# Two unused 64-byte buffers, one ahead of and one behind the halves of the down and mixer weights

## The reference

```
def swiglu(h, w_gate, w_up, w_down):
    return (jax.nn.silu(h @ w_gate) * (h @ w_up)) @ w_down
```

## Time and profile before

| what | before |
|---|---|
| median of three runs | 1358.2 us |
| profiled execution, its own time | 1359.12 us |
| its span, first to last instruction | 1357.3 us |
| mean granted TensorE clock | 0.971 |
| matrix engine (PE) busy | 94% of the span |
| VectorE (DVE) busy | 77% |
| ScalarE (ACT) busy | 45% |

### The profile page before, as it was taken

One profiled execution on the slowest core, in us unless ns is written; L12 is line 12 of the kernel. 1 busy time (PEld: TensorE's weight loads), 2 busy tenths in 40 slices (PEclk: granted clock), 3 DMA queues, 4 the chain that ended last, 5 costly groups with the idle time before them and its releaser, 6 DMA issues.

```text
span 1357.3 us, 21395 instructions
## 1 busy us (share of the span) xinstructions
PE 1282.4 (94%) x8744; PEld 1167.1 (86%) x8744; DVE 1050.6 (77%) x1380; ACT 608.8 (45%) x868; POOL 136.3 (10%) x156
## 2 busy tenths in 40 slices
PE   1999999999999999999999999999978889899998
PEld 1899998988999998999999889999976667799997
DVE  7789897777878648898877868999469996755554
ACT  4533334566333336443445664333362235634443
POOL 0010000000005100000000000000007770000000
PEclk8899999999999998999999989999989989999999
DMA  9699997442886653999974427444542204355551
GB/s 374 250 365 347 354 360 287 143 153 90 299 311 261 260 189 140 351 342 357 364 290 153 156 69 290 186 186 185 197 144 78 78 16 139 121 201 197 197 196 48
DMA packets 55774, 296.12 MB, mean 218 GB/s; under 512 B 6560, under 2 KB 6816, under 8 KB 32416
## 3 DMA queue, kind: packets, MB, share of 16 engines
q1 hardware_dynamic: 46496, 228.21, 46.0%
q0 software_dynamic: 9216, 67.11, 12.6%
HBM read 294.25 MB, written 1.05 MB: 218 GB/s over the span
## 4 chain that ended last, share of the span: by engine, by line
PE 83%; DVE 11%; ACT 3%; issue 1%; DMA 1%; SPq 0%; DVEq 0%; ACTq 0%
PE gu_bank L541 17%; PE gu_bank L542 16%; PE gu_bank L543 16%; PE y_bank L543 8%; PE y_bank L542 8%; PE y_bank L541 8%; DVE ysc L1766 2%; DVE dn_lo L1369 1%; PE t_bank L541 1%; PE t_bank L543 1%; PE t_bank L542 1%; DVE acc_m L1315 1%; DVE xn L1432 1%; DVE vin L1761 1%; DMA pro<-ada 1%
## 5 line engine op out<-in xcount | busy, mean ns | idle before, releaser
L541 PE MATMUL gu_bank<-hT_hi,gu_hi 128*128 128x256 f32 x1760 | 494.6, 281 | 8.3 <-DVE hT_lo L1356 8.0
L543 PE MATMUL gu_bank<-hT_hi,gu_lo 128*128 128x256 f32 x1760 | 491.2, 279 | 0.0
L542 PE MATMUL gu_bank<-hT_lo,gu_hi 128*128 128x256 f32 x1760 | 491.1, 279 | 0.0
L541 PEld LDWEIGHTS gu_bank<-hT_hi,gu_hi 128*128 128x128 f32 x1760 | 334.2, 190 | 15.7 <-issue 9.6
L542 PEld LDWEIGHTS gu_bank<-hT_lo,gu_hi 128*128 128x128 f32 x1760 | 334.8, 190 | 5.4 <-issue 1.0
L543 PEld LDWEIGHTS gu_bank<-hT_hi,gu_lo 128*128 128x128 f32 x1760 | 333.7, 190 | 0.0
L1374 DVE TENSOR_TENSOR gu_lo<-raw_gu,gu_hi 128x2048 fp32r<-128x2048 f32 x105 | 241.0, 2295 | 40.5 <-ACT gu_hi L1037 40.5
L1049 ACT ACTIVATE sg<-gu_bank 128x256 f32<-128x256 f32 x110 | 42.3, 385 | 450.0 <-PE gu_bank L543 449.9
L1037 ACT ACTIVATE gu_hi<-raw_gu 128x2048 fp32r<-128x2048 f32 x105 | 201.1, 1915 | 11.9 <-DMA raw_gu<-ffn_gu 11.7
L542 PE MATMUL y_bank<-dn_lo,act_hi 128*128 128x512 f32 x440 | 174.3, 396 | 0.0
L543 PE MATMUL y_bank<-dn_hi,act_lo 128*128 128x512 f32 x440 | 174.2, 396 | 0.0
(11 more groups left out here) (337 smaller groups left out, 1803.6 us busy)
## 6 DMA issues: line engine op xcount, KB each, us to landing
raw_gu<-ffn_gu SPq DMA_DIRECT2D x110, 1024.0 KB, 6.0
stage<-ada POOLq DMA_DIRECT2D x64, 1024.0 KB, 7.8
raw_dn<-ffn_dn SPq DMA_DIRECT2D x110, 512.0 KB, 3.8
ring<-mix_w SPq DMA_DIRECT2D x72, 512.0 KB, 3.7
pro<-ada SPq DMA_DIRECT2D x5, 1024.0 KB, 12.3
gate_b<-gate_rows SPq DMA_DIRECT2D x6, 512.0 KB, 3.8
stage<-ada SPq DMA_DIRECT2D x2, 1024.0 KB, 20.8
x<-x_in SPq DMA_DIRECT2D x1, 1024.0 KB, 6.3
```

Of the source, the lines that this page charges most:

```text
L541: pe.matmul(to, a[0], b[0], start=start, stop=False)
L542: pe.matmul(to, a[0], b[1], start=False, stop=False)
L543: return pe.matmul(to, a[1], b[0], start=False, stop=stop)
```

## The change

It adds two buffers of 16 float32 values per partition (64 bytes) that nothing reads or writes. `dn_gap` stands ahead of `dn_hi`, `dn_end` behind `dn_lo`. No instruction, DMA, wait or order is changed.

```
         raw_dn = sb(ctx, "raw_dn", [P, 2, D])
+        sb(ctx, "dn_gap", [P, 16])
         dn_hi = sb(ctx, "dn_hi", [P, SLOTS, D], F32R)
         dn_lo = sb(ctx, "dn_lo", [P, SLOTS, D], F32R)
+        sb(ctx, "dn_end", [P, 16])
         ring = sb(ctx, "ring", [P, RING, D])
```

## The result

The changed kernel takes 1377.4 us (median of 4 runs, 1375.5 to 1378.2), the kernel before 1357.7 us in the runs beside it. The ratio is 1.0139, with a 95% interval of 1.0122 to 1.0157. The profiled execution took 1376.89 us with a span of 1375.1 us.

The account below looks back on a forecast made before the run. The prediction took PE's distance between matmul starts to bound the kernel. Its terms, −7.0 − 3.1 + 0.4 + 2.2 − 0.2 = −7.7 us, took 1358.2 to 1350.5 us; range 1344.0 to 1371.0, the forecast's own 1343.5 to 1354.5.

Parts of the forecast that it names:

- What bounds the kernel: PE bounds it, busy 94% of the span; in feed-forward parts time is matmul count times distance between starts.
- Step 6: Gate-up, 5280 matmuls in the feed-forward parts, keeps its places modulo 128 and so its time: 0 us.
- Step 1: Down's operands become equal modulo 128, 233.3 to 226.8 ns over 1320 matmuls: 7.0 us gained.
- Step 2: Input products become unequal modulo 128, from 120.0 ns to between 113.3 and 117.7 ns: 3.1 us gained.
- Step 3: Query and key products, 192 matmuls, become equal modulo 128, 117.8 to 120.0 ns: 0.4 us lost.
- Step 4: Output products and the second part's value products, 336 matmuls, become unequal modulo 128: 2.2 us lost.
- Step 5: Value products in the first part's mixers, 24 matmuls, become equal modulo 128: 0.2 us gained.
- Step 7: VectorE and ScalarE instructions change by 6 and 17 ns each, hidden behind PE: costed at 0.
- step 8: DMAs: ring and later buffers move by 128 bytes, raw_gu and raw_dn stay: costed at 0.
- The first rival: Gate-up falls into its slower 117.7 ns rhythm: +19.5 us on the forecast's −7.7, 1370.0 us; chance 0.32.
- two ways: Gate-up slows because down hands over at another phase, or because its stationary operand lies 64 behind under a 256-byte period.

Follow-up runs that it names:

- sweep: No model work, only matmul streams at all 64 pairs of stationary and moving places in 64-byte steps: 113.3 to 120.0 ns for 256 columns.
- third experiment: Changed kernel without dn_end, so gate-up's stationary operand lies 128 from its moving one modulo 256 (g = 128): 1379.2 us.
- first experiment: Changed kernel with dn_end at 48 numbers instead of 16, so the buffers from ring on lie 256 bytes on instead of 128: 1367.2 us.
- 2 x 2: Against the kernel before, stationary less moving place modulo 256 set for gate-up (g) and down (d) to (64, 128) and (192, 64): 1357.6 and 1379.5 us.
- second experiment: Kernel before with only the buffers from ring on moved by 128 bytes, dn_hi and dn_lo unmoved (g = 192, d = 192): 1362.3 us.
- eleventh: No model work, matmul blocks at ten kernels' places, all 64 placements, then changed kernel's places with one extra matmul ahead of gate-up: 113.3 or 117.8 ns.
- 1353.6 us kernel: Kernel of the first experiment with act_hi and act_lo 192 bytes further on (g = 64, d = 192): 1353.6 us, ratio 0.9966.

## Why the prediction was wrong

- *What bounds the kernel* was right, and so was the reading that placement acts through the distance of matmuls. The rule of the Trainium skill, "SBUF — State Buffer", section "Who interferes with whom" ("PE and ACT never wait on anyone"), read as the prediction read it, does not hold for these streams: with matmuls alone running, distances differ by up to 6.7 ns with place alone (113.3 to 120.0 ns). The formula that the prediction takes from the Trainium skill, "TensorE: Matmul & The Clock Gate", section "Back-to-back issue gap", is given there for a matmul by itself, without a budget for the weight loads that these streams have, so it was no measure of them.
- *Step 6, gate-up at 0*, is the step that failed. It held that gate-up "keeps its places modulo 128". The period is 256 (sweep, and g = 128 in the third experiment), and against `hT` the later buffers had moved by half of it. Measured: +17.9 us.
- *Step 1, down 7.0 us gained*, failed for the same reason. I called the new pair equal; modulo 256 it is 128 apart, at 232.7 ns. Operands that really are equal give the forecast 226.7 ns (first experiment), but gate-up then fell into the slower rhythm and the kernel still lost 9 us.
- *Step 2*, the middle between two rhythms, 3.1 us, was measured at 3.1 us, with both rhythms present; that they mixed to the middle is luck. Step 3 forecast +0.4 and measured +0.3, for another reason than it gave: the operands are 128 apart, not equal. Step 4 forecast 2.2 and measured 0.7, since 192 apart is 229 ns and not 233. Step 5's 0.2 us, over 24 matmuls, is too small to be told. Step 7 held: VectorE was busy 1052.0 us against 1050.6 and ScalarE 607.9 against 608.8. So did step 8: from 60 to 140 us PE is busy all 80.00 us in both kernels, with the DMA engines at 0.92 after and 0.93 before. In the forecast's own range the 0.2 us of step 5 is counted twice; it should run from −3.5 to −14.5 us.
- *The first rival* had the right place (gate-up in its slower rhythm) and nearly the right price: 19.5 us forecast, 17.9 measured. Its sum of 1370.0 was too low since I let the 7.0 us of step 1 stand in it. With that at nothing it is 1377.0, and 1377.4 was measured; that they lie so close is in part luck, since the products of the table add up to only 15.7 us. Of its two ways, the experiments give part to each. With d at 64 or 128 it takes g = 192 to be slow (the 2 x 2), but g = 192 is not slow by itself (40 blocks in the second experiment, the extra matmul in the eleventh). What runs ahead of gate-up can decide with every address of gate-up unmoved: 117.7 ns in the first experiment and 113.8 ns in the 1353.6 us kernel, between which only `act` moved. With 0.32 on this rival and a range to 1371, I trusted a period that the trace had already put in doubt, by 113.3 against 117.8 ns for two pairs that are the same modulo 128.

What stays open is the mechanism inside SBUF, and a rule for which entry leads to which rhythm. The places of the operands do not suffice: the streams of the eleventh experiment gave the places of the kernel before both rhythms, and the places of the 1353.6 us kernel, fast as a whole kernel, only the slower one. Why the changed kernel's down and g = 192 together always lead to the slower rhythm is therefore not shown.

## What to carry to other kernels

Where one engine's streams run back to back, read the distance from start to start, not the duration, and look for like instructions with two distances. Before moving any buffer, list how each stationary operand lies to its moving one modulo 256 bytes, before and after, also for the buffers that a pad pushes along. A fast rhythm may hang on how the stream is entered, so a local gain (226.7 ns for down) can cost more in the stream behind it, and a placement has to be timed in the whole kernel, over many runs.

## What the runs showed of the hardware

With float32 in the engine's fast form at full clock, the distance from one matmul to the next depends on the difference of its two operands' places modulo 256 bytes: 256 columns at 113.3, 117.8, 118.7 or 120.0 ns, 512 columns at 226.7, 228.9, about 233 or 233.3 ns, with nothing but matmuls running. At the same addresses a stream of 256 columns has two rhythms, 113.3 and 117.8 ns, at differences of 64 and of 192. In the profiled whole kernels it kept one through the matmuls of down between its blocks, over more than 60 us, until an interruption; with matmuls alone it also changed between one block and the next without one.
